# Second unit pair of each feed-forward stage in PSUM banks 4 to 7, its weight splits ahead of the first eviction

## The chip, the cores and the metric

The kernel runs on one core of one Trainium2 chip. The metric is the device time of one execution in microseconds (us), the median over runs. A core has a matrix engine (PE, TensorE), a vector engine (DVE), a scalar engine (ACT), GpSimd (POOL) and a queue engine (SP) that issues transfers. Matmul results land in PSUM, which has eight banks; everything else here lives in SBUF.

## The reference, cut to what matters

One inference step of a two-layer decoder trunk over 576 tokens (512 prompt, 64 sample), model width 1024, float32. Each layer is half a SwiGLU, a mixer, half a SwiGLU; the mixer is retention in the first layer and sparse attention in the second, with a shared key/value projection between them.

```python
def rmsnorm(x, g):
    y = x32 * lax.rsqrt(jnp.mean(x32 * x32, axis=-1, keepdims=True) + EPS)
    return (y * g.astype(jnp.float32)).astype(x.dtype)

def swiglu(xn, w_in, w_out):            # w_in 1024 x 5632, w_out 2816 x 1024
    a, b = jnp.split(xn @ w_in, 2, axis=-1)
    return (jax.nn.silu(a) * b) @ w_out

for layer in range(DEPTH):              # DEPTH = 2
    x = x + 0.5 * swiglu(rmsnorm(x, ffn_norm[layer, 0]), ffn_w_in[layer, 0], ffn_w_out[layer, 0])
    x = x + mix                         # retention, or sparse attention
    x = x + 0.5 * swiglu(rmsnorm(x, ffn_norm[layer, 1]), ffn_w_in[layer, 1], ffn_w_out[layer, 1])
```

So there are four feed-forward stages. The program's list of stages is ffn0, ret, ffn1, kv, ffn2, nsa, ffn3, with norm number m from 0 to 6.

## The kernel before, in words

Every projection is worked through in *units*. A unit is one block of weights, 128 output features by all 1024 inputs (`UA`), or by 1408 inputs in the second product of a feed-forward stage (`UB`). Units alternate between two SBUF slots, 0 and 1, of `w_staged`. SP loads unit u+2 into a slot when both splits of unit u are done (`load`). ACT then copies the block to `w_high` in a rounded format (`split_high`, L303), and DVE subtracts to get the rest, `w_low` (`split_low`, L308). The activations are split in the same way (`xh_f`, `xl_f`). PE takes three passes per 128 inputs, high by high, high by low, low by high, each over two halves of 288 tokens (`passes`, L421): 48 matmuls, in 24 pairs, for a unit of size `UA`.

A feed-forward stage goes in two halves (h = 0, 1) of `FH` = 11 *pairs* of units and 8 output units each. The even unit of a pair gives the gate, in PSUM banks 0 and 1; the odd one gives the value, in banks 2 and 3. For a pair DVE multiplies the gate by 1/rms (L545), which counts `free[0]` up; ACT applies SiLU (L508); DVE multiplies by the value (L549), by 1/rms (L551), and splits the result (L552, L553). Between these stand the splits of the next pair's weights: on ACT both behind the SiLU, on DVE the even unit's behind L545 and the odd unit's behind L553. PE may start the next even unit when its `w_low` is there and the gate of the pair before has left its banks (`take_block`: `lo_ready`, `free`).

Four counters order this. `w_used` counts units that PE has finished; `split_high(u)` waits until it is u-1, so that PE is done with unit u-2, whose slot is overwritten. `sq_sum` says that the mean of the squares is in PSUM, `root_ready` that ACT has taken its square root (L394), `r_ready` that DVE has inverted it (L414).

At a stage's start the norm and the first pair run together (`first_pair_pe`): units 0 and 1 are interleaved, unit 1 three steps behind, as the pieces of x are split. The mean of the squares is one product with a matrix of ones (`mean_pe`, L344), in banks 5 and 6. It stands at step k = 4 of the interleaving, in ffn0 at k = 7, just behind unit 0's last pass. Stage ffn2 uses the norm of the stage before it (`KEPT`), and has no mean, root or reciprocal.

Of the kernel before, what the change touches and what calls it, by code (L numbers as in the profile page):

```python
# [111 lines left out]
def trunk_program(nc, a, o):  # L112

    with ExitStack() as ctx:
# [224 lines left out]

        def mean_pe(pe, m):  # L340

            pe.wait_ge(sq_used, 7 * roots_before(m) + 7)
            for h in range(2):
                mm = pe.matmul(ps[:, 5 + h, 0:HALF], ones_v, r[:, h * HALF:(h + 1) * HALF], start=True, stop=True)  # L344
            mm.then_inc(sq_sum, 1)
# [21 lines left out]
        def norm_act(act, n, m, xh, g0):  # L367
# [9 lines left out]
            else:  # L377
# [12 lines left out]
                for k in range(2 if m in SQUARED else 1, KT):  # L390
                    high(act, xh, g0, k)
            if m != KEPT:
                act.wait_ge(sq_sum, n + 1)
                act.activation(wide(r[:, :]), bank2(5), ACT.Sqrt, bias=gain[:, G_EPS:G_EPS + 1]  # L394
                               ).then_inc(root_ready, 1)

        def norm_dve(dve, cv, n, m, xh, xl, g0):
# [6 lines left out]
            for k in range(KT):  # L404
# [5 lines left out]
                if m in SQUARED and k == 1:  # L410
                    split_low(dve, U0[STAGES[m]] + 1, 1, UA)
            if m != KEPT:
# [38 lines left out]
        def unit_pe(pe, u, slot, uses, nk, hi, lo, between=None):  # L451

            take_block(pe, u, slot, uses)
            for k in range(nk):
                mm = passes(pe, 2 * slot, slot, k * P, hi[:, k, :], lo[:, k, :], k == 0, k == nk - 1)
# [14 lines left out]
        def ffn_pe(pe, f, s, n, m):  # L470
            for h in range(2):
# [5 lines left out]

                def outs(i):
# [3 lines left out]
                if h == 0:  # L482
                    first_pair_pe(pe, ub, (f0, f1), xh_f, xl_f, m)
                else:
                    pair(0)
                with pe.Fori(1, FH) as j:
# [12 lines left out]
        def ffn_act(act, ca, f, s, n, m, last):  # L499
            stored(act, f)  # L500
            norm_act(act, n, m, xh_f, G_FFN + 8 * f)
            for h in range(2):
                ub = U0[s] + 30 * h

                def pair(j, size):
# [3 lines left out]
                    split_high(act, u + 2, 0, size)  # L509
                    split_high(act, u + 3, 1, size)  # L510
# [14 lines left out]
                pair(0, UA)  # L525
# [8 lines left out]
        def ffn_dve(dve, cv, f, s, n, m, last):  # L534
            stored(dve, f)
            norm_dve(dve, cv, n, m, xh_f, xl_f, G_FFN + 8 * f)
            for h in range(2):
                ub, f0, f1 = U0[s] + 30 * h, F0[s] + 15 * h, F1[s] + 15 * h

                def pair(j, size):  # L540
# [4 lines left out]
                    dve.tensor_tensor(wide(sg[:, :]), bank2(0), wide(r[:, :]), ALU.mult).then_inc(free[0], 1)  # L545
                    split_low(dve, u + 2, 0, size)
                    dve.wait_ge(w_used, u + 2)
                    dve.wait_ge(sg_ready, FH * (2 * f + h) + j + 1)
                    dve.tensor_tensor(wide(hf[:, :]), wide(sg[:, :]), bank2(2), ALU.mult).then_inc(free[1], 1)  # L549
# [5 lines left out]
                    split_low(dve, u + 3, 1, size)  # L555
# [16 lines left out]
                cv.loop(FH - 1, 2, lambda j: pair(j, UA))  # L572
# [1869 lines left out]
```

## Time and profile before

| | |
|---|---|
| median of 3 runs | 3047.63 us (3046.9 to 3055.93) |
| the profiled execution, first to last instruction | 3039.4 us |
| PE busy | 2879.1 us, 95% |
| PE weight loads busy | 2658.8 us, 87% |
| DVE busy | 1373.4 us, 45% |
| ACT busy | 761.3 us, 25% |
| POOL busy | 205.9 us, 7% |
| mean granted TensorE clock | 0.969 of full speed |
| DMA | 287.59 MB, mean 95 GB/s |

The times of the trace are those of one profiled execution, from its first instruction; its 3039.4 us stand beside a median of 3047.63 us for whole runs, which also hold what lies before the first and behind the last instruction. A row of the trace gives the start, how long the instructions of the row took together, how many there are (x2 is two), and in square brackets how long the engine had been idle and who ended that. PE is the engine to look at: where it has no gap and its granted clock (PEclk) is 1.00, nothing that another engine does costs time.

### The profile page before, as it was taken

The page shows a single profiled execution, that of the slowest core. Times are in us where ns is not written, and L with a number is a line of the kernel's source. Part 1 is how long each engine was busy: PE and PEld are TensorE (multiplying, and loading weights), DVE is VectorE, ACT ScalarE, POOL GpSimd, SP SyncE. Part 2 cuts the span into 40 slices and gives each one's busy share as a digit, 9 for nine tenths or more (in the row PEclk, how much of TensorE's full clock was granted, in tenths as well). Part 3 has the DMA queues.
Part 4 walks back from the last instruction along what each step waited for, and adds up shares of the span by engine and source line. Part 5 has one row for each costly group of instructions (what it writes and reads, how often), then busy time and mean ns, then how long its engine had stood idle before and what let it go on. Part 6 is the DMA issues. An engine that isn't in the chain of part 4 may idle for free.

```text
span 3039.4 us, 52577 instructions
## 1 busy us (share of the span) xinstructions
PE 2879.1 (95%) x21282; PEld 2658.8 (87%) x21282; DVE 1373.4 (45%) x1999; ACT 761.3 (25%) x1163; POOL 205.9 (7%) x298
## 2 busy tenths in 40 slices
PE   7999999999999799999998999999979967999999
PEld 7999998787887699999977999999955546999999
DVE  4434433536354544344522442445458844543342
ACT  3212223222212322122213221223135522321121
POOL 0000003212121000000001000000010032000000
PEclk9999999999999899999999999999869989999999
DMA  3222222334242333222334222222140054222222
GB/s 105 83 90 76 85 88 97 129 111 156 83 167 63 118 89 93 75 83 95 108 133 157 70 93 73 83 92 70 49 146 1 2 181 146 76 79 87 76 88 89
DMA packets 83120, 287.59 MB, mean 95 GB/s; under 512 B 10464, under 2 KB 18720, under 8 KB 82352
## 3 DMA queue, kind: packets, MB, share of 16 engines
q1 hardware_dynamic: 64224, 212.37, 22.6%
q0 software_dynamic: 18768, 73.42, 7.0%
q8 instruction: 93, 1.52, 0.2%
q14 instruction: 35, 0.29, 0.0%
HBM read 260.97 MB, written 33.16 MB: 97 GB/s over the span
## 4 chain that ended last, share of the span: by engine, by line
PE 85%; DVE 6%; issue 2%; DMA 2%; ACT 2%; POOL 1%; POOLq 1%; ACTq 0%; SPq 0%; DVEq 0%
PE ps L421 70%; PE ps L638 4%; PE ps L1259 1%; DVE att_stats L1712 1%; PE ps L1235 1%; DVE probs L1724 1%; PE ps L689 1%; PE ps L1614 1%; PE ps L1495 1%; DVE probs_T L1734 1%; DMA out_state_s<-sample_state 1%; DMA sample_state<-in_state 1%; ACT w_high L303 1%; PE ps L1112 1%; PE ps L1600 1%
## 5 line engine op out<-in xcount | busy, mean ns | idle before, releaser
L308 DVE TENSOR_TENSOR w_low<-w_staged,w_high 128x1024 fp32r<-128x1024 f32 (+1 forms) x334 | 443.3, 1328 | 541.7 <-ACT w_high L303 540.8
L303 ACT ACTIVATE w_high<-w_staged 128x1024 fp32r<-128x1024 f32 (+1 forms) x334 | 372.4, 1115 | 1079.8 <-PE ps L421 934.3
L421 PE MATMUL ps<-xh_f,w_high 128*128 128x288 f32 x2816 | 608.8, 297 | 33.7 <-DVE xl_f L401 25.3
L421 PE MATMUL ps<-xl_f,w_high 128*128 128x288 f32 x2816 | 606.7, 296 | 0.0
L421 PE MATMUL ps<-xh_f,w_low 128*128 128x288 f32 x2816 | 606.2, 296 | 0.0
L421 PEld LDWEIGHTS ps<-xh_f,w_high 128*128 128x128 f32 x2816 | 454.7, 190 | 37.1 <-issue 28.1
L421 PEld LDWEIGHTS ps<-xl_f,w_high 128*128 128x128 f32 x2816 | 455.2, 190 | 0.0
L421 PEld LDWEIGHTS ps<-xh_f,w_low 128*128 128x128 f32 x2816 | 454.6, 190 | 0.0
L421 PE MATMUL ps<-hh,w_low 128*128 128x288 f32 x1408 | 301.5, 295 | 0.0
L421 PE MATMUL ps<-hl,w_high 128*128 128x288 f32 x1408 | 301.4, 295 | 0.0
L421 PE MATMUL ps<-hh,w_high 128*128 128x288 f32 x1408 | 301.4, 295 | 0.0
L421 PEld LDWEIGHTS ps<-hl,w_high 128*128 128x128 f32 x1408 | 225.7, 188 | 0.0
L421 PEld LDWEIGHTS ps<-hh,w_low 128*128 128x128 f32 x1408 | 225.7, 188 | 0.0
L421 PEld LDWEIGHTS ps<-hh,w_high 128*128 128x128 f32 x1408 | 225.6, 188 | 0.0
L508 ACT ACTIVATE silu_gate<-silu_gate 128x576 f32<-128x576 f32 x88 | 60.4, 686 | 541.3 <-DVE silu_gate L545 541.3
L545 DVE TENSOR_TENSOR silu_gate<-ps,rstd 128x576 f32<-128x576 f32 x88 | 66.7, 758 | 211.9 <-PE ps L421 211.6
L549 DVE TENSOR_TENSOR h_full<-silu_gate,ps 128x576 f32<-128x576 f32 x88 | 66.4, 754 | 211.2 <-PE ps L421 211.2
L565 DVE SCALAR_TENSOR_TENSOR x<-ps,x 128x576 f32<-128x576 f32 (+1 forms) x64 | 48.3, 755 | 196.8 <-PE ps L421 196.8
L421 PE MATMUL ps<-xh_r,w_high 128*128 128x288 f32 x512 | 112.0, 300 | 9.5 <-ACT ret_v L789 7.5
L421 PE MATMUL ps<-xl_r,w_high 128*128 128x288 f32 x512 | 109.6, 295 | 0.0
L421 PE MATMUL ps<-xh_r,w_low 128*128 128x288 f32 x512 | 109.2, 295 | 0.0
L421 PEld LDWEIGHTS ps<-xh_r,w_high 128*128 128x128 f32 x512 | 81.5, 188 | 14.5 <-issue 13.6
(368 smaller groups left out, 3721.4 us busy)
## 6 DMA issues: line engine op xcount, KB each, us to landing
w_staged<-in_wa SPq DMA_DIRECT2D x270, 512.0 KB, 3.6
w_staged<-in_wb SPq DMA_DIRECT2D x64, 704.0 KB, 4.1
sample_state<-in_state POOLq DMA_DIRECT2D x32, 512.0 KB, 7.1
out_state_s<-sample_state POOLq DMA_DIRECT2D x32, 512.0 KB, 4.3
cmp_pages<-in_pages_cmp POOLq DMA_DIRECT2D x36, 256.0 KB, 4.7
cmp_pages<-in_pages_cmp SPq DMA_DIRECT2D x28, 256.0 KB, 4.4
k_pages<-in_pages_k SPq DMA_DIRECT2D x32, 128.0 KB, 3.7
v_pages<-in_pages_v POOLq DMA_DIRECT2D x32, 128.0 KB, 4.1
```

Source lines behind the costliest of these rows:

```text
L303: act.activation(wh[:, slot, 0:size], wf[:, slot, 0:size], ACT.Copy).then_inc(hi_ready, 1)
L308: dve.tensor_tensor(wl[:, slot, 0:size], wf[:, slot, 0:size], wh[:, slot, 0:size].bitcast(F32), ALU.subtract).then_inc(lo_ready, 1)
L421: mm = pe.matmul(ps[:, out + h, 0:HALF], w[:, slot, cols:cols + P], m[:, h * HALF:(h + 1) * HALF], start=(first and n == 0), stop=(last an ...
L508: act.activation(sg[:, :], sg[:, :], ACT.Silu).then_inc(sg_ready, 1)
L545: dve.tensor_tensor(wide(sg[:, :]), bank2(0), wide(r[:, :]), ALU.mult).then_inc(free[0], 1)
L549: dve.tensor_tensor(wide(hf[:, :]), wide(sg[:, :]), bank2(2), ALU.mult).then_inc(free[1], 1)
L565: dve.scalar_tensor_tensor(t, bank2(2 * k), 0.5, t, ALU.mult, ALU.add).then_inc(free[k], 1)
L638: mm = pe.matmul(ps[0:m, 4 + t if t < 4 else 0, :], xx[:, k, c0:c0 + m], w[:, i % 2, kk * DV:(kk + 1) * DV], start=(k == 0 and n == 0), st ...
L689: mm = pe.matmul(ps[:, bank + j, :], km[rows, 2 * (j % 2) + odd, t * P:(t + 1) * P], rv[rows, 4, :], start=True, stop=True)
L1112: mm = pe.matmul(ps[:, (b0, b1)[b], at], rot, part[:, j % 2, cols], start=True, stop=True)
L1235: mm = pe.matmul(ps[0:m, 4 + t if t < 4 else 0, :], xx[:, k, c0:c0 + m], w[:, i % 2, kk * 512:(kk + 1) * 512], start=(k == 0 and n == 0), ...
L1259: mm = pe.matmul(ps[:, SLOTS[e % 2][v], 0:G * ch], w1[:, v, t, :], rhs, start=(t == 0), stop=(t == 7))
```

## The change

In the first half (h = 0) of each feed-forward stage the second pair (units 2 and 3) is computed into banks 4 to 7 in place of 0 to 3 (`pair_apart` on PE). Unit 2 no longer waits for `free[0]`; unit 3 waits for `root_ready` instead, since the mean of the squares now stands in its banks 6 and 7 (`MEAN = 6`). DVE reads that pair from banks 4 and 6, and its first two pairs are written out ahead of the loop. The weight splits move too. In ffn0 the splits of units 2 and 3 stand ahead of the square root on ACT and ahead of the reciprocal on DVE (`ahead`). In ffn1, ffn2 and ffn3 unit 2's splits stand behind the root and the reciprocal and ahead of the first pair's eviction; unit 3's stay where they were.

```diff
+        MEAN = 6
         def mean_pe(pe, m):
             pe.wait_ge(sq_used, 7 * roots_before(m) + 7)
             for h in range(2):
-                mm = pe.matmul(ps[:, 5 + h, 0:HALF], ones_v, r[:, h * HALF:(h + 1) * HALF], start=True, stop=True)
+                mm = pe.matmul(ps[:, MEAN + h, 0:HALF], ones_v, r[:, h * HALF:(h + 1) * HALF],
+                               start=True, stop=True)
...
@@ norm_act
+            if m == 0:
+                ahead()
             if m != KEPT:
                 act.wait_ge(sq_sum, n + 1)
-                act.activation(wide(r[:, :]), bank2(5), ACT.Sqrt, bias=gain[:, G_EPS:G_EPS + 1]
+                act.activation(wide(r[:, :]), bank2(MEAN), ACT.Sqrt, bias=gain[:, G_EPS:G_EPS + 1]
...
@@ norm_dve
+            if m == 0:
+                ahead()
             if m != KEPT:
                 dve.wait_ge(root_ready, n + 1)
                 dve.reciprocal(r[:, :], r[:, :]).then_inc(r_ready, 1)
...
@@ ffn_pe
+                def pair_apart():
+                    unit_pe(pe, ub + 2, 0, 0, KT, xh_f, xl_f, bank=4)
+                    if m != KEPT:
+                        pe.wait_ge(root_ready, n + 1)
+                    unit_pe(pe, ub + 3, 1, 0, KT, xh_f, xl_f, bank=4)
...
                 if h == 0:
                     first_pair_pe(pe, ub, (f0, f1), xh_f, xl_f, m)
+                    pair_apart()
                 else:
                     pair(0)
-                with pe.Fori(1, FH) as j:
+                with pe.Fori(2 - h, FH) as j:
                     pair(j)
...
@@ ffn_act
+            def ahead():
+                split_high(act, U0[s] + 2, 0, UA)
+                split_high(act, U0[s] + 3, 1, UA)
+
+            norm_act(act, n, m, xh_f, G_FFN + 8 * f, ahead)
+            if m:
+                split_high(act, U0[s] + 2, 0, UA)
...
                     act.activation(sg[:, :], sg[:, :], ACT.Silu).then_inc(sg_ready, 1)
-                    split_high(act, u + 2, 0, size)
-                    split_high(act, u + 3, 1, size)
+                    if done < 1:
+                        split_high(act, u + 2, 0, size)
+                    if done < 2:
+                        split_high(act, u + 3, 1, size)
...
-                pair(0, UA)
+                pair(0, UA, 0 if h else 1 if m else 2)
...
@@ ffn_dve
+            def ahead():
+                split_low(dve, U0[s] + 2, 0, UA)
+                split_low(dve, U0[s] + 3, 1, UA)
+
+            norm_dve(dve, cv, n, m, xh_f, xl_f, G_FFN + 8 * f, ahead)
+            if m:
+                split_low(dve, U0[s] + 2, 0, UA)
...
-                    dve.tensor_tensor(wide(sg[:, :]), bank2(0), wide(r[:, :]), ALU.mult).then_inc(free[0], 1)
-                    split_low(dve, u + 2, 0, size)
+                    dve.tensor_tensor(wide(sg[:, :]), bank2(bank), wide(r[:, :]), ALU.mult).then_inc(free[0], 1)
+                    if done < 1:
+                        split_low(dve, u + 2, 0, size)
...
-                    dve.tensor_tensor(wide(hf[:, :]), wide(sg[:, :]), bank2(2), ALU.mult).then_inc(free[1], 1)
+                    dve.tensor_tensor(wide(hf[:, :]), wide(sg[:, :]), bank2(bank + 2), ALU.mult
+                                      ).then_inc(free[1], 1)
...
-                    split_low(dve, u + 3, 1, size)
+                    if done < 2:
+                        split_low(dve, u + 3, 1, size)
...
-                cv.loop(FH - 1, 2, lambda j: pair(j, UA))
+                if h == 0:
+                    pair(0, UA, 0, 1 if m else 2)
+                    pair(1, UA, 4)
+                    cv.loop(FH - 3, 2, lambda j: pair(j + 2, UA))
+                else:
+                    cv.loop(FH - 1, 2, lambda j: pair(j, UA))
```

On ACT at the start of ffn0, this stands before, and then after the change (in brackets the semaphores waited for: `block_used` is `w_used`, `squares_mean` is `sq_sum`, `slot0_free` is `free[0]`):

```order
L394 ACT_TABLE_LOAD
L394 ACTIVATE rstd<-ps,gain 128x576 [waits squares_mean]
L508 ACT_TABLE_LOAD
L508 ACTIVATE silu_gate<-silu_gate 128x576 [waits slot0_free]
L303 ACTIVATE w_high<-w_staged 128x1024 [waits block_used,block_landed_0]
L303 ACTIVATE w_high<-w_staged 128x1024 [waits block_used,block_landed_1]
```

```order
L303 ACTIVATE w_high<-w_staged 128x1024 [waits block_used,block_landed_0]
L303 ACTIVATE w_high<-w_staged 128x1024 [waits block_used,block_landed_1]
L399 ACT_TABLE_LOAD
L399 ACTIVATE rstd<-ps,gain 128x576 [waits squares_mean]
L529 ACT_TABLE_LOAD
L529 ACTIVATE silu_gate<-silu_gate 128x576 [waits slot0_free]
```

Both high splits have moved ahead of the square root and of the table load that it needs; the second of them waits for unit 1.

On DVE at the same place, the reciprocal and the first pair's work before, with the loop's entry (L105) between, and after:

```order
L414 RECIPROCAL rstd<-rstd 128x576 [waits root_ready]
L105 UNCONDITIONAL_BRANCH [waits rstd_ready]
L105 ISA
L544 REGISTER_ALU [waits block_used]
L545 TENSOR_TENSOR silu_gate<-ps,rstd 128x576 [waits h_split_ready]
L307 REGISTER_ALU
L308 TENSOR_TENSOR w_low<-w_staged,w_high 128x1024 [waits w_high_ready]
```

```order
L308 TENSOR_TENSOR w_low<-w_staged,w_high 128x1024 [waits w_high_ready] x2
L421 RECIPROCAL rstd<-rstd 128x576 [waits root_ready]
L575 TENSOR_TENSOR silu_gate<-ps,rstd 128x576 [waits block_used,rstd_ready]
L580 TENSOR_TENSOR h_full<-silu_gate,ps 128x576 [waits silu_ready,block_used]
L583 TENSOR_TENSOR h_full<-h_full,rstd 128x576 [waits slot1_free]
L584 CAST hh<-h_full 128x576 [waits vector_steps]
L585 TENSOR_TENSOR hl<-h_full,hh 128x576 [waits vector_steps]
L575 TENSOR_TENSOR silu_gate<-ps,rstd 128x576 [waits h_split_ready,block_used]
```

Two low splits now stand ahead of the reciprocal, and the second pair's gate follows the first pair without a split between.

On ACT at the start of ffn1 (ffn2 and ffn3 alike), before and after:

```order
L394 ACTIVATE rstd<-ps,gain 128x576 [waits squares_mean]
L508 ACT_TABLE_LOAD
L508 ACTIVATE silu_gate<-silu_gate 128x576 [waits slot0_free]
L303 ACTIVATE w_high<-w_staged 128x1024 [waits block_used,block_landed_0]
L303 ACTIVATE w_high<-w_staged 128x1024 [waits block_used,block_landed_1]
```

```order
L399 ACTIVATE rstd<-ps,gain 128x576 [waits squares_mean]
L303 ACTIVATE w_high<-w_staged 128x1024 [waits block_used,block_landed_0]
L529 ACT_TABLE_LOAD
L529 ACTIVATE silu_gate<-silu_gate 128x576 [waits slot0_free]
L303 ACTIVATE w_high<-w_staged 128x1024 [waits block_used,block_landed_1]
```

Unit 2's high split has moved ahead of the table load and the SiLU, behind the square root.

## Rows read from the trace of the kernel before

**Rows 1.** Page, chain that ended last: share by engine.
```profile
...
PE 85%; DVE 6%; issue 2%; DMA 2%; ACT 2%; POOL 1%; POOLq 1%; ACTq 0%; SPq 0%; DVEq 0%
...
```

**Rows 2.** Waits of PE, whole span: us in total, times, longest.
```profile
...
PE ps L421 <- DVE w_low L308: 8.4, 4, 5.5
...
```

**Rows 3.** Chain, 0 to 60: start, us, what.
```profile
...
29.59 0.75 ACT rstd L394
...
30.36 3.76 DVE rstd L414
...
34.45 0.77 DVE silu_gate L545
...
35.83 1.05 ACT w_high L303
...
36.91 1.24 DVE w_low L308
...
```

**Rows 4.** PE in order of time, ffn0: start, us, instructions.
```profile
...
32.25 0.42 PE L421 MATMUL ps<-xh_f,w_low 128*128 128x288 f32 x2
38.19 0.85 PE L421 MATMUL ps<-xh_f,w_high 128*128 128x288 f32 x2 [5.51 <-DVE w_low L308]
...
52.96 0.43 PE L421 MATMUL ps<-xh_f,w_high 128*128 128x288 f32 x2
...
```

**Rows 5.** DVE in order of time, ffn0.
```profile
...
38.05 0.75 DVE L549 TENSOR_TENSOR h_full<-silu_gate,ps 128x576 f32<-128x576 f32 x1
...
40.32 0.76 DVE L553 TENSOR_TENSOR hl<-h_full,hh 128x576 f32 x1
...
46.85 0.76 DVE L545 TENSOR_TENSOR silu_gate<-ps,rstd 128x576 f32<-128x576 f32 x1 [4.63 <-PE ps L421]
```

**Rows 6.** ACT in order of time, ffn0.
```profile
...
47.64 0.69 ACT L508 ACTIVATE silu_gate<-silu_gate 128x576 f32<-128x576 f32 x1 [9.82 <-DVE silu_gate L545]
...
```

**Rows 7.** Windows: length, each engine's busy time, PEclk, DMA.
```profile
...
38.19:42.42 4.23, 4.23 (x18) 4.23 (x18) 3.72 (x5) 0.00 (x0) 0.00 (x0) 0.50 0.41 124
...
```

**Rows 8.** PE in order of time, ffn1.
```profile
...
1045.10 0.51 PE L421 MATMUL ps<-xh_f,w_high 128*128 128x288 f32 x2 [1.99 <-DVE xl_f L401]
...
1062.42 0.43 PE L421 MATMUL ps<-xh_f,w_low 128*128 128x288 f32 x2
...
1064.31 0.42 PE L421 MATMUL ps<-xl_f,w_high 128*128 128x288 f32 x2
...
```

**Rows 9.** PE in order of time, ffn2.
```profile
...
1683.53 0.43 PE L421 MATMUL ps<-xh_f,w_low 128*128 128x288 f32 x2
...
1685.07 0.43 PE L421 MATMUL ps<-xl_f,w_high 128*128 128x288 f32 x2
...
```

**Rows 10.** PE in order of time, ffn3.
```profile
...
2609.37 0.50 PE L421 MATMUL ps<-xh_f,w_high 128*128 128x288 f32 x2 [1.81 <-DVE xl_f L401]
...
2624.72 0.43 PE L421 MATMUL ps<-xh_f,w_low 128*128 128x288 f32 x2
...
2626.59 0.42 PE L421 MATMUL ps<-xl_f,w_high 128*128 128x288 f32 x2
...
```

**Rows 11.** DVE in order of time, ffn1.
```profile
...
1055.67 3.75 DVE L414 RECIPROCAL rstd<-rstd 128x576 f32<-128x576 f32 x1 [3.50 <-ACT rstd L394]
...
```

**Rows 12.** Windows: the starts of ffn1 and ffn3, and a busy stretch.
```profile
...
1046.00:1052.80 6.80, 6.24 (x26) 5.68 (x25) 6.05 (x8) 4.54 (x7) 0.00 (x0) 0.50 0.27 80
1080.00:1460.00 380.00, 380.00 (x2925) 380.00 (x2924) 157.72 (x177) 79.35 (x82) 0.00 (x0) 1.00 0.28 85
2609.37:2622.40 13.03, 11.76 (x81) 11.08 (x82) 10.61 (x11) 8.63 (x11) 0.00 (x0) 1.00 0.13 40
...
```

**Rows 13.** ACT in order of time, in kv.
```profile
...
1657.58 1.28 ACT L1126 ACT_TABLE_LOAD   x1
1658.87 0.42 ACT L1126 ACTIVATE token_stats<-ps,gain 126x4 f32<-126x4 f32 x2
```

**Rows 14.** Page, DMA issues: KB each, us to landing.
```profile
...
w_staged<-in_wa SPq DMA_DIRECT2D x270, 512.0 KB, 3.6
...
```

More of the change, by code:

```diff
@@ L365, in high, with norm_act @@
             act.activation(xh[:, k, :], x[:, k, :], ACT.Copy, scale=gain[:, g0 + k:g0 + k + 1]).then_inc(xh_ready, 1)
-        def norm_act(act, n, m, xh, g0):
+        def norm_act(act, n, m, xh, g0, ahead=None):
             if m == 0:
@@ L391, in norm_act, with norm_dve @@
                     high(act, xh, g0, k)
+            if m == 0:
+                ahead()
             if m != KEPT:
                 act.wait_ge(sq_sum, n + 1)
-                act.activation(wide(r[:, :]), bank2(5), ACT.Sqrt, bias=gain[:, G_EPS:G_EPS + 1]
+                act.activation(wide(r[:, :]), bank2(MEAN), ACT.Sqrt, bias=gain[:, G_EPS:G_EPS + 1]
                                ).then_inc(root_ready, 1)
-        def norm_dve(dve, cv, n, m, xh, xl, g0):
+        def norm_dve(dve, cv, n, m, xh, xl, g0, ahead=None):
             def low(k):
@@ L449, in first_pair_pe, with unit_pe @@
             mm.then_inc(w_used, 1)
-        def unit_pe(pe, u, slot, uses, nk, hi, lo, between=None):
+        def unit_pe(pe, u, slot, uses, nk, hi, lo, between=None, bank=0):
             take_block(pe, u, slot, uses)
             for k in range(nk):
-                mm = passes(pe, 2 * slot, slot, k * P, hi[:, k, :], lo[:, k, :], k == 0, k == nk - 1)
+                mm = passes(pe, bank + 2 * slot, slot, k * P, hi[:, k, :], lo[:, k, :], k == 0, k == nk - 1)
                 if between and k < nk - 1:
@@ L500, in ffn_act, with pair @@
             stored(act, f)
-            norm_act(act, n, m, xh_f, G_FFN + 8 * f)
+            def ahead():
[4 more added lines that the diff above has]
+                split_high(act, U0[s] + 2, 0, UA)
             for h in range(2):
                 ub = U0[s] + 30 * h
-                def pair(j, size):
+                def pair(j, size, done=0):
                     u = ub + 2 * j
@@ L535, in ffn_dve, with pair @@
             stored(dve, f)
-            norm_dve(dve, cv, n, m, xh_f, xl_f, G_FFN + 8 * f)
+            def ahead():
[4 more added lines that the diff above has]
+                split_low(dve, U0[s] + 2, 0, UA)
             for h in range(2):
                 ub, f0, f1 = U0[s] + 30 * h, F0[s] + 15 * h, F1[s] + 15 * h
-                def pair(j, size):
+                def pair(j, size, bank=0, done=0):
                     u = ub + 2 * j
```

## The prediction

> **What bounds the kernel now.** I read the page's chain first: 85% of the chain that ended last is PE [rows 1]. So a change is worth what it takes out of PE's gaps, and what it saves or costs in the half-speed stretches that follow gaps. Next PE's waits: the group that the change aims at, the product L421 held up by `w_low` (L308), is 8.4 us in four waits, the longest 5.5 [rows 2]. That is one wait in each feed-forward stage, and it caps the direct gain near 8.4 us, 0.3% of the time. The chain of ffn0's start shows what the longest is made of: root, reciprocal, gate eviction, SiLU, high split, low split, each started by the one before [rows 3]. Between the matmul pairs at 32.25 and 38.19 PE does nothing [rows 4], and the 4.23 us behind the gap ran at a granted clock of 0.50 [rows 7], which is 1.2 GHz in place of 2.4. Elsewhere in these stages PE has no gap: from 1080 to 1460 it is busy 380.00 of 380 us [rows 12]. That is 2925 matmuls, so 0.13 us each, 0.26 a pair, 6.24 a unit.
>
> **ffn0, before.** Unit 1's last pair starts at 32.25, so the next could start at 32.51. Unit 2 starts at 38.19, unit 4 at 52.96 [rows 4]; the 14.8 between these two are 2 x 6.24 = 12.5 for two units, 4.23/2 = 2.1 for the half clock [rows 7], and 0.2 of slightly wider pairs.
>
> **ffn0, after.** Unit 2 goes to free banks, and its splits need only unit 0, whose last pass stands four steps before unit 1's end (four steps x 3 pairs x 0.26 = 3.1 us, and the mean's four matmuls). They take 1.05 and 1.24 [rows 3], on idle engines, and are done before 32.5. So PE goes straight on. Units 2 and 3 then last until 32.51 + 12.5 = 45.0, if nothing holds unit 3.
>
> But the second high split waits for unit 1, and the root stands behind it on ACT, with its table load. Step by step:
> - unit 1's end 32.25 + 0.42 = 32.67 [rows 4], high split 1.05 [rows 3]: 33.8
> - table load 1.28, work right behind it [rows 13]: 35.1
> - root 0.75, reciprocal 3.76 with the hand-over [rows 3]: 35.9, then 39.65. Root and reciprocal end 5.5 us later than before. Unit 3 waits for the root (35.9) and for its low split (33.8 + 1.24 = 35.1): both long before 38.75, hidden.
> - first gate eviction: before it came 34.45 - 30.36 = 4.09 behind the reciprocal's start [rows 3], 0.33 of it beyond the 3.76, part of which was the loop's entry, now further on. I take 39.8
> - SiLU 0.79 behind the eviction's start (46.85 [rows 5] to 47.64 [rows 6]) and 0.69 long: 41.3
> - value product to the end of the activation's split: 38.05 to 40.32 + 0.76 = 3.03 [rows 5]: 44.35. No weight split stands between now; two left this chain, 2.5 us
> - second gate eviction 44.4. Its matmuls (unit 2) ended at 38.75, so DVE is late here, not PE
> - eviction to high split of unit 4: 35.83 - 34.45 = 1.38; high to low split 36.91 - 35.83 = 1.08 [rows 3]; low split to PE 38.19 - 36.91 = 1.28 [rows 3, 4]. Unit 4 starts at 48.15.
>
> Unit 4's weights come behind unit 2's low split, near 31, and land in about 3.6 us [rows 14]: hidden. So unit 4 starts 52.96 - 48.15 = 4.8 us earlier, but PE has stood still from 45.0 to 48.15: the stall of 5.5 has not gone, it has moved two units on and shrunk to 3.15. The next units are covered: unit 5's low split ends some 4.2 us behind unit 4's start, unit 4 lasts 6.24.
>
> *What the clock does behind a stall of 3.15.* Not shown, so bounded by the nearest rows. Behind 5.5 us idle: 4.23 us at half speed, 2.1 lost. In ffn1 behind 1.99 idle [rows 8]: 6.80 at 0.50 with PE busy 6.24 of them, 3.1 lost; in ffn3 behind 1.81 idle [rows 10]: 1.00 throughout, nothing lost [rows 12]. Bounds 0 and 3.1; I take 2.1, the same stage's own. ffn0's net: 4.8 - 2.1 = 2.7.
>
> The Trainium skill ("TensorE: Matmul & The Clock Gate", Part 1) says that the array's default is the half rate, that activity lifts it, and that the instant depends on a monitor running free of the kernel. By it the fall behind this stall is likely and its length a matter of luck; the rows (3.1 lost behind 1.99, nothing behind 1.81) agree.
>
> **ffn1, ffn2, ffn3.** Start of the pair before the gap to the second pair behind it, less two pairs of 0.26: 1.89 - 0.52 = 1.37 [rows 8], 1.54 - 0.52 = 1.02 [rows 9], 1.87 - 0.52 = 1.35 [rows 10]. Together 3.7. All three go if unit 2's low split is ready by unit 1's end. In ffn1 the next pair is due at 1062.68. Unit 0 ended four steps earlier, 1062.68 - 3.12 = 1059.56, plus 0.16 to run out; high split 1.05, low split 1.24, so near 1062.1. The reciprocal ahead of the low split ends at 1055.67 + 3.75 = 1059.4 [rows 11], not in the way. Margin 0.6; ffn3 the same, ffn2 has no reciprocal. What is late next: the eviction now waits behind this low split on DVE, from about 1060 to 1062. The SiLU's table load, now behind the high split, ends by 1062.1 too: hidden. From the eviction, 0.79 + 0.69 + 3.03 + 1.24 gives unit 3's low split near 1067.8; unit 3 is due at 1062.68 + 6.24 = 1068.9. Margin 1.1, so no new gap.
>
> **Edits at nothing.** The mean in banks 6 and 7: same matmuls, same readers; in ret, kv and nsa nothing else moves. The 384 matmuls written out in the pairs apart (96 a stage) replace loop turns. Evictions from banks 4 and 6 are of the same shape.
>
> **Sum.** 2.7 + 3.7 = 6.4 us less. Against the profiled execution, 3039.4 - 6.4 = 3033.0 from first to last instruction. The median of the runs before lies 8.2 above that span; the change touches nothing there, so 3047.6 - 6.4 = 3041.2, 0.21% less. What can be told from no change is 0.3%, 9.1 us.
>
> **Rivals.**
> 1. *The clock does not fall behind the new stall.* For: 1.81 us idle did not make it fall. Against: 3.15 is longer than the 1.99 that did. Then 4.8 + 3.7 = 8.5 less: 3039.1.
> 2. *The table load costs more when the root waits on it.* In the trace the work follows 0.01 us behind its 1.28 [rows 13], so in this kernel a switch on the path costs 1.3. A mechanism that made ACT stand another table load's time would move unit 4 on to about 49.4: 4.8 - 1.3 - 2.1 + 3.7 = 5.1 less: 3042.5. The Trainium skill ("ScalarE: Activation LUTs", What ACT_TABLE_LOAD costs) has such a rule: it adds a drain of about 1.38 us to 1.28 for each switch. By it, an estimate, the gain would be near 5.0. Rows 13 speak against it: the square root there starts at once.
> 3. *Low-clock stretches elsewhere shift.* Everything behind ffn0 comes some microseconds earlier, and whether a short gap at a stage's start brings a fall seems to hang on its instant. ffn1's 3.1 could vanish, or ffn3 could get such a fall: 3.3 to 9.5 less, 3044.3 to 3038.1, with more if it meets rival 1.
> 4. *Slower: PE's instructions come late at the loop's entry.* Before, PE entered the loop of pairs under the stall at unit 2; now it enters at unit 4 with the array busy in three of four stages, behind 96 more matmuls of straight code. If a block of instructions were not there it would take about a transfer, 3.6 us [rows 14], and a gap of that length the 2.1 of half clock: 4 x 5.7 = 22.8, less 6.4, is 16.4 more, 3064.0. It decides from 1.6 us a stage. Against: 1080 to 1460 holds ffn1's second half with the same entry behind straight code, with no gap [rows 12].
> 5. *The split ahead does nothing in ffn0*, if units 2 and 3 hung on the root after all. By the steps above they don't, with 2.9 us to spare: under 1 in 50, taken with rival 4.
>
> **How the numbers follow.** Forecast 0.55, rival 1 0.16, rival 2 0.07, rival 3 0.16, rivals 4 and 5 0.06. Faster by over 9.1 us needs rival 1 or a lucky rival 3, or both: 0.20. Slower by over 9.1 us is rival 4: 0.05. The rest, 0.75, lies within 0.3%. The range takes in rivals 1 to 3 with 3 us of luck on the good side and nearly no gain on the other: 3036 to 3047.
>
> **What would show it.** In the profile after, PE has no gap between units 1 and 2 in any feed-forward stage. In ffn0 the root starts near 35.1 in place of 29.59, the second gate eviction near 44.4, and PE waits for `w_low` once, about 3 us, before unit 4 near 48.2, with about 4 us at 0.50 behind. PE's waits on `w_low` total about 3 in place of 8.4. It is wrong if PE stalls at unit 3 of ffn1 to ffn3, if unit 4 of ffn0 starts before 47 or behind 49.5, or if a gap of PE has no `w_low` to blame.

## The result, and the profile after

| | before | after |
|---|---|---|
| median, 20 runs each | 3052.89 us (3041.2 to 3059.94) | 3034.72 us (3011.03 to 3048.09) |
| ratio | | 0.9946, 95% interval 0.9931 to 0.9961 |
| profiled execution, first to last instruction | 3039.4 us | 3031.8 us |

The change takes 0.54% off, 16 us (12 to 21). That is faster by more than 0.3%, which had a chance of 0.20; the forecast was 6.4 us, 0.21%. The measured 3034.72 lies 1.3 us below the forecast's range of 3036 to 3047. That range was worked out from a median of 3047.63 for the kernel before, which twenty runs put at 3052.89, so as a saving the miss is larger: 16 us against 11.6 at the range's good end. Two things stand out: the gain is more than twice what the starts of the stages hold, and the runs scatter more than before, with a standard deviation of 9.8 us against 6.1.

The chain that ended last is again mostly PE's, by the page of the kernel after:

```profile
...
PE 86%; DVE 6%; DMA 2%; issue 2%; ACT 2%; POOL 1%; POOLq 1%; ACTq 0%; SPq 0%; DVEq 0%
...
```

PE's waits on weights, whole span (us in total, times, longest):

```profile
...
PE ps L428 <- DVE w_low L308: 2.8, 1, 2.8
...
```

One wait of 2.8 is left of four with 8.4 together [rows 2]. PE in ffn0, where L428 is the product, in order of time:

```profile
...
32.15 0.42 PE L428 MATMUL ps<-xh_f,w_high 128*128 128x288 f32 x2
...
44.37 0.42 PE L428 MATMUL ps<-xh_f,w_low 128*128 128x288 f32 x2
47.60 0.54 PE L428 MATMUL ps<-xh_f,w_high 128*128 128x288 f32 x2 [2.81 <-DVE w_low L308]
...
48.77 0.66 PE L428 MATMUL ps<-xl_f,w_high 128*128 128x288 f32 x2
...
52.42 0.43 PE L428 MATMUL ps<-xh_f,w_high 128*128 128x288 f32 x2
...
```

PE runs through from unit 1 into unit 2, where it stood 5.5 us before [rows 4]: 48 pairs every 0.26 from 32.15 lead to 44.63. Then it waits for unit 4's low split until 47.60. Inside ffn0 the five breaks seen in profiles of this start (this kernel, after_again, ffn0_only, met_wait_unit2 and tiny_wait_unit2) are alike, 2.5 to 2.8 us. ACT and DVE over the same stretch, in order of time:

```profile
...
28.32 1.06 ACT L303 ACTIVATE w_high<-w_staged 128x1024 fp32r<-128x1024 f32 x1 [4.41 <-PE ps L428]
32.41 1.06 ACT L303 ACTIVATE w_high<-w_staged 128x1024 fp32r<-128x1024 f32 x1 [3.03 <-PE ps L428]
33.49 1.28 ACT L399 ACT_TABLE_LOAD   x1
34.78 0.74 ACT L399 ACTIVATE rstd<-ps,gain 128x576 f32<-128x576 f32 x1
...
```

```profile
...
35.56 3.75 DVE L421 RECIPROCAL rstd<-rstd 128x576 f32<-128x576 f32 x1 [0.83 <-ACT rstd L399]
39.35 0.76 DVE L575 TENSOR_TENSOR silu_gate<-ps,rstd 128x576 f32<-128x576 f32 x1
...
43.87 0.76 DVE L575 TENSOR_TENSOR silu_gate<-ps,rstd 128x576 f32<-128x576 f32 x1
46.32 1.23 DVE L308 TENSOR_TENSOR w_low<-w_staged,w_high 128x1024 fp32r<-128x1024 f32 x1 [1.70 <-ACT w_high L303]
...
```

The second high split waits for unit 1's end, the table load and the root follow it back to back, the reciprocal starts at 35.56 in place of 30.36 [rows 3], and the second gate eviction at 43.87 is late. Windows of the gap and of what follows it (length, busy times of PE, PEld, DVE, ACT, POOL, granted clock, DMA):

```profile
...
44.79:47.60 2.81, 0.00 (x1) 0.00 (x1) 1.28 (x2) 2.44 (x3) 0.00 (x0) 1.00 0.00 0
48.80:52.10 3.30, 3.30 (x16) 3.30 (x15) 2.55 (x4) 0.00 (x0) 0.00 (x0) 0.50 0.53 159
...
```

So the clock fell to its lower level (0.50, 1.2 GHz) for 3.3 us behind a gap of 2.81 us.

In ffn1 there is no gap at unit 2. DVE there, where before the reciprocal was followed by the first eviction:

```profile
...
1055.12 3.75 DVE L421 RECIPROCAL rstd<-rstd 128x576 f32<-128x576 f32 x1 [3.58 <-ACT rstd L399]
1060.24 1.23 DVE L308 TENSOR_TENSOR w_low<-w_staged,w_high 128x1024 fp32r<-128x1024 f32 x1 [1.37 <-ACT w_high L303]
1061.38 0.75 DVE L575 TENSOR_TENSOR silu_gate<-ps,rstd 128x576 f32<-128x576 f32 x1
...
1065.71 1.22 DVE L308 TENSOR_TENSOR w_low<-w_staged,w_high 128x1024 fp32r<-128x1024 f32 x1
1068.38 0.76 DVE L575 TENSOR_TENSOR silu_gate<-ps,rstd 128x576 f32<-128x576 f32 x1 [1.45 <-PE ps L428]
...
```

Unit 2's low split ends at 1061.47, and PE's first pair of unit 2 starts at 1061.94, 0.26 us behind the last of unit 1, without a stop. Unit 3's low split ends at 1066.93, and unit 3 starts at 1068.18.

### The profile page after: what moved, and what is told of

Same layout as the page of the kernel before. It is cut to its first block, busy times and chain, and to the rows that moved or that the text cites. A ratio compares the mean times of both kernels' runs of the same rounds, so it can differ in the third digit from the quotient of the medians.

```text
span 3031.8 us, 52492 instructions
## 1 busy us (share of the span) xinstructions
PE 2874.1 (95%) x21282; PEld 2657.4 (88%) x21282; DVE 1373.2 (45%) x1999; ACT 761.3 (25%) x1163; POOL 205.5 (7%) x298
## 4 chain that ended last, share of the span: by engine, by line
PE 86%; DVE 6%; DMA 2%; issue 2%; ACT 2%; POOL 1%; POOLq 1%; ACTq 0%; SPq 0%; DVEq 0%
PE ps L428 70%; PE ps L676 4%; DVE att_stats L1750 1%; PE ps L1297 1%; PE ps L1273 1%; DVE probs L1762 1%; PE ps L727 1%; PE ps L1652 1%; PE ps L1533 1%; DVE probs_T L1772 1%; DMA out_state_s<-sample_state 1%; DMA sample_state<-in_state 1%; PE ps L1150 1%; PE ps L1143 1%; DMA cmp_pages<-in_pages_cmp 1%
## 5 line engine op out<-in xcount | busy, mean ns | idle before, releaser
L428 PE MATMUL ps<-xh_f,w_high 128*128 128x288 f32 x2816 | 608.9, 297 | 27.0 <-DVE xl_f L406 24.1
L428 PE MATMUL ps<-xl_f,w_high 128*128 128x288 f32 x2816 | 607.1, 297 | 0.0
L428 PE MATMUL ps<-xh_f,w_low 128*128 128x288 f32 x2816 | 606.7, 296 | 0.0
L428 PEld LDWEIGHTS ps<-xh_f,w_high 128*128 128x128 f32 x2816 | 455.2, 190 | 29.8 <-issue 24.2
L428 PEld LDWEIGHTS ps<-xl_f,w_high 128*128 128x128 f32 x2816 | 455.9, 190 | 0.0
L428 PEld LDWEIGHTS ps<-xh_f,w_low 128*128 128x128 f32 x2816 | 455.2, 190 | 0.0
L428 PE MATMUL ps<-hh,w_low 128*128 128x288 f32 x1408 | 301.4, 295 | 0.0
L428 PE MATMUL ps<-hl,w_high 128*128 128x288 f32 x1408 | 301.3, 295 | 0.0
L428 PE MATMUL ps<-hh,w_high 128*128 128x288 f32 x1408 | 301.3, 295 | 0.0
L428 PEld LDWEIGHTS ps<-hl,w_high 128*128 128x128 f32 x1408 | 225.7, 188 | 0.0
L428 PEld LDWEIGHTS ps<-hh,w_high 128*128 128x128 f32 x1408 | 225.7, 188 | 0.0
L428 PEld LDWEIGHTS ps<-hh,w_low 128*128 128x128 f32 x1408 | 225.6, 188 | 0.0
L428 PE MATMUL ps<-xh_r,w_high 128*128 128x288 f32 x512 | 111.8, 299 | 9.5 <-ACT ret_v L827 7.5
L428 PE MATMUL ps<-xl_r,w_high 128*128 128x288 f32 x512 | 109.5, 295 | 0.0
L428 PE MATMUL ps<-xh_r,w_low 128*128 128x288 f32 x512 | 109.4, 295 | 0.0
L428 PEld LDWEIGHTS ps<-xh_r,w_high 128*128 128x128 f32 x512 | 81.6, 188 | 14.4 <-issue 11.9
```

What stands on the lines that cost most here:

```text
L428: mm = pe.matmul(ps[:, out + h, 0:HALF], w[:, slot, cols:cols + P], m[:, h * HALF:(h + 1) * HALF], start=(first and n == 0), stop=(last an ...
```

## What the starts alone explain

From the first product behind ffn0's mean to the reciprocal of the stage ret it took 431.3 us in the profile before (29.18 to 460.44) and 427.8 after (28.82 to 456.65): 3.4 us less. The gaps of ffn1 to ffn3 were worth 3.7. That is 7.1 us, close to the forecast, and to the two spans, 7.6 apart. Over many runs the change is worth 16. Some 9 us had to come from something that these two profiles have alike or show too little of.

A candidate shows when matmuls are counted in equal stretches inside the four stages. Here the kernel before, 300 us inside each of ffn0, ffn1, ffn2 and ffn3 (PE's busy time and its count first):

```profile
...
100.00:400.00 300.00, 300.00 (x2252) 300.00 (x2251) 121.42 (x138) 60.40 (x62) 0.00 (x0) 1.00 0.27 84
1100.00:1400.00 300.00, 300.00 (x2310) 300.00 (x2309) 128.78 (x147) 61.30 (x63) 0.00 (x0) 1.00 0.28 86
1750.00:2050.00 300.00, 300.00 (x2252) 300.00 (x2251) 120.77 (x136) 58.99 (x61) 0.00 (x0) 1.00 0.27 85
2700.00:3000.00 300.00, 300.00 (x2252) 300.00 (x2251) 118.86 (x133) 57.35 (x57) 0.00 (x0) 1.00 0.27 85
...
```

PE is busy throughout and at full clock in all four, and yet does 2310 matmuls in ffn1 and 2252 in the others: a pair every 0.260 us, or every 0.2667. No records are missing that could feign this: every profile but that of ones_each_pair, which has added products, holds 21282 matmuls. From start to start the two look different. At the fast pace the steps go 132, 128, 132, 128 ns; at the slow one every fourth matmul comes 140 ns behind the one before it, and the others 130 to 132. The passes repeat every six matmuls, so it is not one of them that is slow. Each stage has 1584 pairs, so a whole stage at the fast pace is worth some 10 us. The theory for the experiments ("the pace"): a stage has one of two paces, the fast one comes up by chance and is lost at the first break of PE's stream; the change takes away the break at unit 2, and so lets it last. Its rival ("the starts"): only the gaps count, and the rest of the 16 us is chance. A third candidate, the granted clock in the stages between, had no experiment of its own; what the record holds on it stands behind the experiments.

## The experiments

Each ratio is to runs of the kernel before made beside it on the same chip (17 to 23 of them for the experiments, medians 3049.41 to 3052.43), so it is not the quotient of two medians of this table. The last column says which pace each of the four stages held in its loops in that kernel's one profile (F fast, s slow).

| kernel | runs | median us | ratio to before, 95% | std. dev. us | ffn0..3 |
|---|---|---|---|---|---|
| before | 20 | 3052.89 | | 6.1 | s F s s |
| before_again | 1 | 3053.66 | | | s s s s |
| after | 20 | 3034.72 | 0.9946 (0.9931-0.9961) | 9.8 | s F s s |
| after_again | 9 | 3037.68 | 0.9957 (0.9936-0.9977) | 7.3 | s F s s |
| ffn0_only | 12 | 3049.05 | 0.9983 (0.9971-0.9995) | 4.7 | s s s s |
| ffn123_only | 6 | 3039.46 | 0.9950 (0.9934-0.9966) | 4.2 | s s s s |
| tiny_wait_unit2 | 12 | 3046.21 | 0.9998 (0.9977-1.0019) | 3.1 | s s s s |
| met_wait_unit2 | 12 | 3036.53 | 0.9952 (0.9927-0.9977) | 9.8 | s s s s |
| root_between | 6 | 3031.97 | 0.9923 (0.9906-0.9940) | 7.6 | s s s s |
| root_between_2 | 12 | 3027.62 | 0.9938 (0.9913-0.9962) | 8.7 | s F s F |
| low3_early | 12 | 3028.83 | 0.9938 (0.9914-0.9962) | 9.3 | s F s F |
| low3_early_2 | 6 | 3023.75 | 0.9908 (0.9880-0.9935) | 5.3 | F s s s |
| break_each_pair | 1 | 3148.04 | | | s s s s |
| ones_each_pair | 1 | 3085.77 | | | s s s s |

**Halves of the change.** A list of stages decides where the pair apart and its splits are used; all else is the kernel after. The edit is cut to PE's part; the same list guards the splits on ACT and DVE and the banks that DVE reads.

```diff
+        APART = (0,)          # ffn0_only; (2, 4, 6) in ffn123_only
-                    pair_apart()
+                    if m in APART:
+                        pair_apart()
+                    else:
+                        pair(1)
```

> The change in ffn0 alone (pair apart and both splits ahead of the root there; ffn1 to ffn3 as before, with a gap of about 1 us ahead of unit 2). Theory of the starts: only the starts count, so 2.7 to 4.8 us less than before, ratio 0.9985 to 0.9991. Theory of the pace: within a feed-forward stage PE runs matmul pairs either every 0.266 or every 0.260 us for the whole stage (10 us between them), drawn at the last restart of PE; the change takes restarts away in ffn1 to ffn3 and so shifts the odds there. By it this kernel keeps the odds of before in three stages, so it lies near 3 to 5 us less too, and the runs scatter over some 20 us as before.

> The change in ffn1, ffn2 and ffn3 alone; ffn0 as before, with the stall of 5.5 us at unit 2. Theory of the starts: 3.7 us less, ratio 0.9988. Theory of the pace: the extra drop of about 10 us belongs to these three stages, so 12 to 15 us less, ratio near 0.9955, with runs scattered over 30 us or more.

> The changed kernel again, to see how its runs scatter beside those of before on one chip. Theory of the starts: 6 to 8 us less, ratio 0.9975 to 0.998. Theory of the pace: near 0.9946 as measured, with a spread of 30 us, and stages at either pace in the profile.

Measured: ffn0 alone gives 5 us (0.9983), as its start says within the interval. The other three stages give 15 us (0.9950), where their gaps hold 3.7. So the surplus is real and is brought by the edits in ffn1 to ffn3; the theory of the starts is out for them. That it also arises inside these stages doesn't follow, and this kernel's own profile doesn't show it: all four stages are at the slow pace there. Its six runs scattered over 11 us, where I had expected 30 or more. The kernel after, again, gives 0.9957: the first measurement was no accident.

**A break of a third of a microsecond, and a wait without one.** Each of two kernels adds one wait of PE ahead of unit 2: tiny_wait_unit2 in ffn1, ffn2 and ffn3, met_wait_unit2 in ffn1 and ffn3.

```diff
                 def pair_apart():
+                    if m:                                # tiny_wait_unit2
+                        pe.wait_ge(free[0], f0 + 1)
+                    if m and m != KEPT:                  # met_wait_unit2, in its place
+                        pe.wait_ge(r_ready, n + 1)
```

> The changed kernel, but in ffn1, ffn2 and ffn3 PE waits at unit 2 for the first gate eviction (free[0]), which ends about 0.15 us behind unit 1's last matmul: a break of 0.1 to 0.4 us in place of none. Theory of the starts: 3 x 0.15 to 0.4, at most 1 us slower than the changed kernel. Theory of the pace, where a break behind the mean has worse odds than none: near 5 to 10 us slower than the changed kernel, ratio to before 0.997 to 0.999.

> The changed kernel with a wait at the same instruction as in the run with the tiny wait (PE at unit 2, in ffn1 and ffn3), but on the reciprocal (r_ready), which is met some 3 us before: an added wait and no break. Theory of the pace: no different from the changed kernel, ratio to before 0.994 to 0.997, scatter of some 9 us. Rival (a wait there costs by itself, whether or not PE stands still): near the run with the tiny wait, ratio about 0.999 and a scatter of 3 us.

PE of the kernel with the tiny wait in ffn1, in order of time, at the end of unit 1 and the start of unit 2:

```profile
...
1060.95 0.42 PE L428 MATMUL ps<-xl_f,w_high 128*128 128x288 f32 x2
1061.21 0.42 PE L428 MATMUL ps<-xh_f,w_low 128*128 128x288 f32 x2
1061.72 0.54 PE L428 MATMUL ps<-xh_f,w_high 128*128 128x288 f32 x2
1062.09 0.42 PE L428 MATMUL ps<-xl_f,w_high 128*128 128x288 f32 x2
1062.36 0.42 PE L428 MATMUL ps<-xh_f,w_low 128*128 128x288 f32 x2
...
```

From 1061.21 to 1062.09 it is 0.88 in place of 0.52: a break of 0.36 us, which the view of waits doesn't even list. Matmuls ahead of and behind it:

```profile
...
1055.00:1061.20 6.20, 6.20 (x50) 6.20 (x49) 4.83 (x3) 2.34 (x2) 0.00 (x0) 1.00 0.00 0
1064.00:1400.00 336.00, 336.00 (x2522) 336.00 (x2522) 140.63 (x162) 66.88 (x70) 0.00 (x0) 1.00 0.27 83
...
```

Start to start, the pairs of the first stretch come every 0.260 us (the 50 take in those cut by its edges); 2522 in 336 us is one every 0.2667. The fast pace was there, and ended at the break. By the same count the breaks in ffn2 and ffn3 are 0.20 and 0.28 us, together 0.84; in this profile both stages were slow already ahead of them.

Over twelve runs the breaks cost 12 to 16 us by the ratios (0.9998 against 0.9946 and 0.9957), 9 to 12 by the medians, more than the 5 to 10 that I had expected and far more than 0.84, and the scatter falls from 9.8 to 3.1. The wait that is met before PE comes to it costs nothing that can be seen (0.9952, scatter 9.8). So it is the break, not the wait. That the break costs that much is shown by the runs; that it does so by the pace is shown in one profile, and for the other runs inferred from size and scatter.

**What brings the fast pace.** Two kernels made to count, not to be fast.

```diff
                 def pair(j):
+                    if not isinstance(j, int):
+                        pe.wait_ge(free[1], f1 + j)      # break_each_pair
                     unit_pe(pe, ub + 2 * j, 0, f0 + j, KT, xh_f, xl_f)
```

```diff
+                    if not isinstance(j, int):           # ones_each_pair
+                        pe.wait_ge(free[0], f0 + j)      # met in any case
+                        if h == 0:
+                            for g in range(2):
+                                pe.matmul(ps[:, 4 + g, 0:HALF], ones_v, r[:, g * HALF:(g + 1) * HALF],
+                                          start=True, stop=True)
+                        else:
+                            pe.matmul(ps[:, 4, 0:1], ones_v, mcol[:, 0:1], start=True, stop=True)
```

> The changed kernel, but in the loops of pairs PE waits at each even unit until DVE has multiplied by the value of the pair before (L580): a gap of some 0.9 us in PE at 19 places of each feed-forward stage. Meant as a count of draws, not as a better kernel: 76 gaps of 0.9 to 1.2 us make it 70 to 95 us slower. Theory of the pace: behind each gap PE runs anew at 0.260 or 0.266 us a pair and holds that until the next gap, so both values stand side by side within one stage. Rival (the pace belongs to a stage or a run, say to the buffers it reads, not to the last break): one value throughout each stage.

> The changed kernel with more work on PE, to see what sets the pace: in the loop of pairs, ahead of each even unit, PE multiplies by the matrix of ones in plain float32 into bank 4, which nobody reads. In the first halves (h = 0) two products of 288 columns, as the mean of the squares is; in the second halves one product of a single column. No wait is added. Costs some 0.75 us x 36 and 0.3 us x 40, together 35 to 45 us. Theory A (a float32 product in the stream draws the pace anew, and so does the mean): both paces occur behind these products, near half of the draws at 0.260. Theory B (behind the mean it is the first pair's stream, not the product, that matters): 0.266 throughout, as behind the gaps of the run with a break at each pair. If one of the two forms draws the fast pace much more often than the other, it could be used.

The first took 3148.04 us. PE's waits there:

```profile
...
PE ps L428 <- DVE h_full L582: 80.9, 76, 3.3
...
```

76 breaks of 1.0 us and more, 76 stretches of two units behind them, and not one at the fast pace. My expectation that a break draws anew, with both values side by side, was wrong; so was that of the rival. The fast pace stood in this profile in one place, in ffn3 from the mean to the first break. The second took 3085.77 us. Ahead of and behind ffn1's first added product:

```profile
...
1065.30:1085.00 19.70, 19.70 (x154) 19.70 (x153) 11.50 (x10) 6.33 (x7) 0.00 (x0) 1.00 0.23 62
1088.00:1100.00 12.00, 12.00 (x90) 11.84 (x88) 4.19 (x5) 2.25 (x3) 0.00 (x0) 1.00 0.32 89
...
```

Start to start these are a pair every 0.260 us ahead of it and every 0.267 behind: a product in plain float32 in the stream ended the fast pace as a break does. In ffn2, which has no mean, the same happened: fast for 89 pairs up to the first added product, slow behind it. At none of the 76 places did it come up behind an added product, as theory B had it, so theory A fell.

What is left is a count. Ahead of and behind each break, read start to start in all fourteen profiles, a fast stretch met a break or an added product nine times, and its pace never survived. A slow stretch met a break at unit 2 or 4 fifteen times, and once it was fast behind it: in ffn1 of the kernel before, whose loops are the fast ones above.

```profile
...
1054.80:1062.40 7.60, 7.60 (x59) 7.60 (x58) 4.51 (x2) 3.51 (x4) 0.00 (x0) 1.00 0.00 1
1066.00:1080.00 14.00, 14.00 (x110) 14.00 (x109) 6.85 (x9) 2.70 (x3) 0.00 (x0) 1.00 0.32 99
...
```

Right behind the mean the stretch was fast in 15 of 42 stages (5 of 14 in ffn0, 7 in ffn1, 3 in ffn3). So the fast pace comes up at a stage's start about once in three times, and an unbroken stage keeps it. In all profiles the stage's loops were at the fast pace in 1 of 21 stages that had a break at unit 2 or 4 (kernels made to count left out), and in 7 of 27 that had none. Through ffn2, which has no mean, it never lasted in 8 tries. These are small counts, and what sets the pace at a stage's start is not settled.

**A better start for ffn0.** In the kernel after, ffn0 still has its stall of 2.8 us, and with it little chance of the fast pace. In root_between the root stands between the two high splits, the reciprocal between the two low ones.

```diff
             def ahead():
                 split_high(act, U0[s] + 2, 0, UA)
-                split_high(act, U0[s] + 3, 1, UA)
             norm_act(act, n, m, xh_f, G_FFN + 8 * f, ahead)
-            if m:
-                split_high(act, U0[s] + 2, 0, UA)
+            split_high(act, U0[s] + (2 if m else 3), 0 if m else 1, UA)
```

DVE has the same edit. In low3_early unit 3's low split moves on by one more place:

```diff
-            split_low(dve, U0[s] + (2 if m else 3), 0 if m else 1, UA)
+            if m:
+                split_low(dve, U0[s] + 2, 0, UA)
...
                     dve.tensor_tensor(wide(sg[:, :]), bank2(bank), wide(r[:, :]), ALU.mult).then_inc(free[0], 1)
                     if done < 1:
                         split_low(dve, u + 2, 0, size)
+                    if done == 2:
+                        split_low(dve, u + 3, 1, size)
```

> As the changed kernel, but in ffn0 the root stands between the two high splits and the reciprocal between the two low splits. Step by step: high split 2 ends near 29.4, table load to 30.7, root to 31.4, reciprocal to 35.2, high split 3 32.5 to 33.6, low split 3 to 36.4, gate eviction 36.4, second gate eviction 41, unit 4's low split near 44.7, before its turn at 45. So no stall at unit 4 and no fall of the clock: against the changed kernel 2.8 us of stall and about 1.5 of half clock less, 4.3 together. Rival: a wait of unit 3 on the low split behind the reciprocal (36.4 against 38.7 needed) or a stall elsewhere eats it: no difference.

> The version with the root between the two high splits of ffn0 again, for a narrower interval. Theory of the starts: 4.3 us less than the changed kernel, ratio to before near 0.994. If its first ratio of 0.9923 holds, the pace has a part here too, since ffn0 then has no break between its first pair and its end.

> The version with the root between the high splits, and unit 3's low split on DVE moved from ahead of the first gate eviction to right behind it, under the SiLU. The eviction comes 1.1 us sooner, the value product 0.7 us sooner, so unit 4's weights are split 0.7 us sooner. Theory of the starts: in the root_between run at the fast pace unit 4 started 0.1 us late, at the slow pace not at all, so at most 0.1 us is to be had: no difference from root_between. Theory of the pace: that 0.1 us was a break that cost ffn0 its fast pace of 0.260 (its 58 pairs behind the mean ran at it, the 1486 behind the break at 0.267). Without it about half of the runs keep it, some 5 us less on the mean than root_between.

> The version with the low split of unit 3 behind the first gate eviction again: for its interval beside the changed kernel's, and for a profile that may show ffn0 at 0.260 throughout. Theory of the starts plus pace: ratio to before 0.992 to 0.995, 3 to 8 us less than the changed kernel.

> The kernel before once more, for a second profile of it. Theory of the pace: each feed-forward stage has its break of 1 to 5.5 us at unit 2, so at most one of the four stages at 0.260 us a pair.

The kernel before, once more, took 3053.66 and had all four stages at the slow pace. In root_between the stall at unit 4 is gone: the time from ffn0's mean to ret's reciprocal is 425.6 in root_between, 2.2 less than after. I had expected 4.3. Inside ffn0, from its first matmul to its last, it is 426.0 us against 429.9, 3.9 less, close to that. The rest was lost again at the end: from 430 to 460, where ret begins, the granted clock was 0.89 in this profile and 0.94 in that of after, which is some 7 us at the lower level in place of 3.5, worth up to 1.7.

In the second profile of this version ffn0 began fast. PE at unit 4, in order of time:

```profile
...
43.71 0.42 PE L428 MATMUL ps<-xh_f,w_low 128*128 128x288 f32 x2
43.99 0.54 PE L428 MATMUL ps<-xh_f,w_high 128*128 128x288 f32 x2
44.37 0.42 PE L428 MATMUL ps<-xl_f,w_high 128*128 128x288 f32 x2
...
```

The low split came 0.1 us late: 0.66 from 43.71 to 44.37 in place of 0.52. Matmuls ahead of it and behind:

```profile
...
31.00:43.90 12.90, 12.90 (x102) 12.90 (x100) 10.13 (x9) 4.66 (x5) 0.00 (x0) 1.00 0.27 81
46.00:400.00 354.00, 354.00 (x2657) 354.00 (x2657) 144.94 (x164) 70.98 (x73) 0.00 (x0) 1.00 0.28 85
...
```

Start to start the first are a pair every 0.260 us; then 2657 in 354 us, every 0.2667. A break of 0.14 us ended the fast pace, and it didn't come back in this stage. low3_early gives unit 4's split some 0.7 us of room, and in its second profile ffn0 is fast to the end:

```profile
...
31.00:400.00 369.00, 369.00 (x2841) 369.00 (x2840) 159.92 (x179) 79.42 (x83) 0.00 (x0) 1.00 0.28 87
...
```

2841 in 369 us is a pair every 0.26. Mean to reciprocal took 413.3 there, against 425.6 in the two profiles without a stall at the slow pace: 12.3 us. Of these 10 are the pace by the count; part of the rest is the clock, which was 1.00 at ret's start in that profile (420 to 450) and 0.89 in root_between's. Both versions beat the kernel before by more than 0.3%. Their ratios, 0.9923 and 0.9938, and 0.9938 and 0.9908, lie below the 0.9946, 0.9957 and 0.9952 of the kernels with the stall, but the intervals overlap: some 5 us better than after is likely. low3_early over root_between, for which I had expected 5 us, is not shown.

**The granted clock, from the record.** Each run of the experiments and of the kernel after is on record with its span and its mean granted clock. One minus the clock, times the span, is the most that the lower level can have cost (in the profiles PE was busy in some 0.8 of that time). Span times clock is the rest of the time.

| kernel | runs | mean clock | lost, at most, us | span x clock, us: mean, least to most |
|---|---|---|---|---|
| before, beside the experiments | 77 | 0.9676 | 98.8 | 2949.0, 2931 to 2959 |
| after, after_again, met_wait_unit2 | 41 | 0.9696 | 92.1 | 2941.5, 2922 to 2955 |
| tiny_wait_unit2 | 12 | 0.9691 | 94.1 | 2950.6, 2949 to 2954 |

Two things follow. First, between the tiny wait and the kernels without a break in ffn1 to ffn3 nearly all of the difference, 9 of 11 us, is outside the clock, and twelve runs with the tiny wait lie within 5 us there, where the others spread over 33. That is what the theory of the pace asks for: with a break in each stage the fast pace hardly ever lasts. Secondly, between the kernel before and the kernel after, 6.7 us at most, and by the share of 0.8 an estimate of 5, are the clock. That leaves, of a mean gain of some 14, about 9, of which the starts' gaps hold 6.4, and only 2 to 3 for the pace: the kernel before has fast stages too, some of them won behind the break. Much of the clock's part lies in nsa, where nothing was changed. Windows there, of before, before_again, after and after_again in turn:

```profile
...
2150.00:2300.00 150.00, 131.04 (x883) 106.97 (x882) 81.13 (x180) 42.09 (x118) 9.05 (x16) 0.73 0.28 89
2150.00:2300.00 150.00, 132.09 (x834) 109.65 (x833) 75.62 (x159) 37.78 (x102) 9.05 (x16) 0.69 0.29 92
2150.00:2300.00 150.00, 129.07 (x902) 105.08 (x902) 84.31 (x196) 44.93 (x132) 9.02 (x16) 0.76 0.27 88
2150.00:2300.00 150.00, 130.24 (x885) 103.61 (x884) 82.62 (x193) 44.94 (x131) 9.02 (x16) 0.73 0.27 88
...
```

With the lower level at 0.50, 0.73 and 0.69 are 81 and 93 us at it, 0.76 and 0.73 are 72 and 81. Why it is shorter behind the change is not shown, and no run was made to test it.

## Why the prediction was right or wrong

- *PE is the bound; the cap near 8.4 us.* The first half was right. The cap was the wrong part: it counted idle time at the starts, and took the pace of a busy PE at full clock as one number. The same holds for the sentence ahead of the forecast that nothing costs time where PE has no gap and a granted clock of 1.00.
- *ffn0 after: no gap at units 2 and 3, the root pushed behind unit 1, one stall before unit 4.* Right in each step. Root 34.78 (forecast 35.1), reciprocal 35.56 (35.9), first eviction 39.35 (39.8), second 43.87 (44.4), unit 4 47.60 (48.15), all in a profile that began 0.36 us earlier. The stall was 2.81 us by the profile (3.15).
- *Half clock behind it.* 2.1 was taken from the nearest row; 3.3 us at 0.50 cost 1.65. The fall also came in the kernel's other profiles with that stall.
- *ffn1 to ffn3: three gaps gone, 3.7 us.* Right: no wait on `w_low` is left there. Unit 2's split had 0.5 us of room (forecast 0.6), unit 3's 1.2 (1.1).
- *Table load.* 1.28, and the root 0.01 behind it (33.49 to 34.78), on the path this time. The drain that the Trainium skill adds for each switch ("ScalarE: Activation LUTs", What ACT_TABLE_LOAD costs) does not show here; rival 2 is out.
- *Sum.* 6.4 forecast; 7.1 by the profiles' starts; 16 measured. Its two terms were near. The step that failed is that "Sum" has nothing else in it, and two things went in at nothing. One is the pace: I had read 0.26 us a pair from the one stretch of before that was fast, used it for every stage, and noted in ffn0 "0.2 of slightly wider pairs" without asking what they were. Those wider pairs, 0.2667 against 0.26, are 10 us a stage, and a break of a third of a microsecond decides over them: three such breaks take back 9 to 16 us. The stretch in which 380.00 of 380 us were busy hid it, for busy is not the same as fast; the count beside it, 2925, set against the same length in another stage, shows it. The other is the granted clock outside the starts: over whole runs its mean was 0.9676 before and 0.9696 after, some 5 us, and most of what the profiles show of it is in nsa, which the change doesn't touch. How the 9 us beyond the starts divide between the two is an estimate, not a test.
- *Rival 3, low-clock stretches elsewhere shift.* It came true in part: the mean clock rose. It did so in nsa, not at the starts that rival 3 named; there ffn1 kept its stretch at 0.50, and ffn3 got one in the profiles of after and after_again. Whether that is the change's doing or luck is open; it held in all three sets of runs of this kernel (0.9696, 0.9700 and 0.9695). It missed the pace. Rival 1 fell, since the clock did fall. Rival 4 fell: the one gap at the loop's entry, in ffn0, was a wait for `w_low`, and the other stages have none.
- *Chances.* 0.75 was on "within 0.3%", and 0.20 on what came, for reasons (rivals 1 and 3) that hold at best a third of it. The 3 runs known then, with a median of 3047.63, lay 5 us below the 3052.89 of twenty, so even the time of the kernel before was a draw.

## What to carry to other kernels

A gap is not the only thing that an idle engine costs. Count instructions in equal busy stretches at full clock, in every stage that does the same work; if the counts differ, find out what starts and ends the better pace before summing gaps. And where the scatter of runs changes with an edit, something that is drawn by chance has been let in or shut out: one profile of each kernel won't show it. Compare the runs' granted clocks too, before all of a gain is put down to one cause.

## What the runs showed of the hardware

- At a granted clock of 1.00 and with PE without a gap, the same stream of fp32r matmuls of 128x288 with their weight loads ran at 2310 or at 2252 per 300 us. At the slower pace every fourth matmul starts 140 ns behind the one before, the others 130 to 132. A stage whose stream nothing broke kept its pace through some 1550 pairs.
- A break, the shortest 0.14 and 0.36 us (ffn0 in root_between_2, ffn1 with the tiny wait), or small float32 products in between (ones_each_pair), ended the fast pace each time that a trace has it, nine times. None of the 76 breaks of 1.0 us and more in break_each_pair brought it up; one of 1.1 us in ffn1 of the kernel before did.
- A granted clock of 0.50 for 3.3 us followed an idle time of 2.81 us. The mean granted clock of whole runs was 0.9676 in 77 runs of the kernel before and 0.9696 in 41 of the changed one, and in their profiles the most of it is in a stage that no edit touches.
- What decides at a stage's start between the two paces stays open.
